# Seven products for the spatial gate's values, and convolution taps begun behind the first two tiles

## The reference, cut to what matters

```python
proj = rms_norm(h, g_mix_pre) @ w_in          # 1024 x 8192
z_sgu, z_conv, z_pool, z_gate = split(proj)   # 2048, 2048, 1024, 3072 columns

def spatial_gating(z, w_s, b_s, g_v, b_v):    # z = gelu(z_sgu)
    u, v = split(z, 2)
    v = layer_norm(v, g_v, b_v)               # v: 256 x 1024, the "values"
    return u * (w_s applied over tokens in blocks of 128 to v, plus b_s)

def conformer_conv(z, w_dw, b_dw, g_ln, b_ln):
    a, gate = split(z, 2)
    h = a * sigmoid(gate)
    h = depthwise causal convolution of h over tokens, 31 taps, + b_dw
    return silu(layer_norm(h, g_ln, b_ln))

def multiscale_pool(z, w_pool, s_pool):       # window means of 2, 4, 8, 16 tokens minus z,
    ...                                       # then four 256 x 256 products
merged = gate0 * (spatial @ w_sgu_out) + gate1 * (conv @ w_conv_out) + gate2 * (pool @ w_pool_out)
```

## Time and profile before

| | |
|---|---|
| median of 3 runs | 2272.47 us |
| profiled execution | 2274.29 us, span 2272.6 us |
| PE busy | 2067.7 us (91%) |
| DVE busy | 1442.3 us (63%) |
| POOL busy | 723.7 us (32%) |
| ACT busy | 699.2 us (31%) |

### The profile page before, as it was taken

The page is one execution under the profiler, slowest core; times in us unless marked ns, Lnnn a source line. Parts: engine busy times, 40 slices in busy tenths (PEclk is TensorE's granted clock), DMA queues, the critical chain, the costliest instruction groups (busy, mean ns, idle before and its releaser), DMA issues.

```text
span 2272.6 us, 21412 instructions
## 1 busy us (share of the span) xinstructions
PE 2067.7 (91%) x6060; PEld 1085.4 (48%) x6060; DVE 1442.3 (63%) x3261; ACT 699.2 (31%) x1517; POOL 723.7 (32%) x627
## 2 busy tenths in 40 slices
PE   9999999999999999999887878799899988887876
PEld 8864445455867555444332222276554444222222
DVE  3989777665551356667666666522766666666664
ACT  1013102111201214444434334423334344433442
POOL 1252420000000024544444445300254456444442
PEclk9999999999999999999999999999999999999999
DMA  6445444444545359999999999963699999999997
GB/s 230 148 150 186 160 162 148 167 167 169 185 166 211 132 226 374 421 422 421 422 422 421 422 422 422 416 243 139 265 421 421 421 422 421 421 422 422 422 421 323
DMA packets 98443, 703.07 MB, mean 309 GB/s; under 512 B 11136, under 2 KB 11648, under 8 KB 13248
## 3 DMA queue, kind: packets, MB, share of 16 engines
q0 software_dynamic: 73856, 537.17, 57.0%
q1 hardware_dynamic: 20016, 141.04, 17.3%
q10 hardware_dynamic: 4496, 23.92, 2.7%
HBM read 700.51 MB, written 1.05 MB: 309 GB/s over the span
## 4 chain that ended last, share of the span: by engine, by line
PE 44%; DMA 30%; ACT 5%; issue 4%; DVE 2%; POOL 1%; POOLq 0%; DVEq 0%; ACTq 0%; SPq 0%
DMA arena<-uv,expert_index 30%; PE aux L1008 13%; PE acc L573 9%; PE acc L538 7%; PE aux L538 5%; PE aux L857 3%; PE acc L1025 2%; PE acc L927 2%; ACT arena L1538 1%; ACT arena L1541 1%; ACT L1538 1%; POOL arena L1279 1%; ACT L1530 1%; DVE arena L2267 1%; PE acc L904 1%
## 5 line engine op out<-in xcount | busy, mean ns | idle before, releaser
L1008 PE MATMUL aux<-arena 128*128 128x512 f32 x2048 | 1002.7, 618 | 183.7 <-ACT arena L1541 180.3
L1279 POOL DMA_INDIRECT arena<-uv,expert_index x512 | 610.3, 1192 | 970.5 <-PE aux L1008 567.9
L2267 DVE SCALAR_TENSOR_TENSOR arena<-arena 128x1024 f32<-128x1024 f32 x512 | 632.4, 1235 | 412.9 <-DMA arena<-uv,expert_index 412.7
L1008 PEld LDWEIGHTS aux<-arena 128*128 128x128 f32 x2048 | 366.9, 192 | 721.1 <-ACT arena L1541 432.5
L1538 ACT ACTIVATE arena<-ident,dots 128x128 f32<-128x128 f32 x512 | 205.3, 401 | 701.9 <-DVE arena L2267 699.7
L573 PE MATMUL acc<-x,w_ring 128*128 128x256 f32 x1264 | 277.3, 382 | 2.5 <-DVE x L1709 2.3
L573 PEld LDWEIGHTS acc<-x,w_ring 128*128 128x128 f32 x1264 | 242.1, 192 | 36.7 <-DVE x L1709 2.5
L1541 ACT ACTIVATE arena<-arena,gate 128x128 f32<-128x128 f32 x512 | 205.5, 401 | 17.0
L1751 DVE TENSOR_TENSOR first_query_weights<-w_ring 128x1024 f32<-128x1024 f32 (+1 forms) x71 | 85.8, 1208 | 101.0 <-PE aux L538 90.3
L538 PE MATMUL acc<-first_query_weights,arena 128*128 128x512 f32 (+1 forms) x284 | 141.6, 581 | 0.1
L1793 DVE SCALAR_TENSOR_TENSOR arena<-arena,channel_vectors (+1 forms) x240 | 108.6, 531 | 0.2
(11 more groups left out here) (322 smaller groups left out, 1892.7 us busy)
## 6 DMA issues: line engine op xcount, KB each, us to landing
w_ring<-stream SPq DMA_DIRECT2D x133, 1024.0 KB, 4.8
arena<-uv,expert_index POOLq DMA_INDIRECT x512, 14.8
arena<-first_heads ACTq DMA_DIRECT2D x6, 1024.0 KB, 10.0
first_query_weights<-first_heads ACTq DMA_DIRECT2D x4, 1024.0 KB, 9.9
row_vectors<-rows ACTq DMA_DIRECT2D x3, 1024.0 KB, 13.0
scratch<-keys ACTq DMA_DIRECT2D x2, 1024.0 KB, 5.5
arena<-ret_out_held ACTq DMA_DIRECT2D x2, 1024.0 KB, 14.8
x<-first_heads ACTq DMA_DIRECT2D x2, 1024.0 KB, 4.8
```

What stands on the lines that cost most here:

```text
L1008: last = nc.tensor.matmul(AUX[2 * tt + c][:, :], DG[:, slot, :], G[:, row(layer, slot), D + c * 512:D + (c + 1) * 512], start=False, stop= ...
L1279: pool.indirect_dma_start(G[:, row(layer, s % RING), :], None, uv, bass.IndirectOffsetOnAxis(ap=EIDX[:, par, s:s + 1], axis=0),).then_inc( ...
L2267: v.scalar_tensor_tensor(G[:, row(layer, slot), 0:D], G[:, row(layer, slot), 0:D], 1.0, HTM[:, tt, :], ALU.mult, ALU.mult, accum_out=HD[:, ...
```

## The change

* `v` becomes the first seven-unit, number 0 (`SPATIAL_V`); all others move up by one (`GATE = 1`, `BRANCH = 4`). Its weight tiles are laid out for it.
* PE: `token_major(X1, KT, 2)` is replaced by four `seven_step`s, the first with order 5, 4, 3, 1, 6, 2, 7, waiting for the u banks to be stored; then it waits for `first_copied` and the unit's third `banks_read` ahead of the pool branch's products.
* ACT: four evacuations with Gelu from PSUM become `copy_first` and four Gelus in place in VT, as the additions come.
* DVE: the loop is written out, and its order changes: banks 0, 1; taps 0; banks 2, 3; taps 2 with banks 4, 5 ahead of its tap 16; banks 6, 7; taps 4; taps 6 with the values' combines 0, 1, 2 ahead of taps 4, 12 and 28; fold; combine 3 of the values; combine 0 of the first gate unit; `add_products` of the values; combines 1 to 3 of the first gate unit.
* POOL: two waits are renumbered to the same points of the work.

```diff
-SEVEN_UNITS = [(first_block("gates") + STEPS * u, STEPS, 512) for u in range(6)]
-BRANCH = 3
+SEVEN_UNITS = [(first_block("v"), STEPS, 512)]
+SPATIAL_V, GATE = 0, 1
+SEVEN_UNITS += [(first_block("gates") + STEPS * u, STEPS, 512) for u in range(6)]
+BRANCH = GATE + 3
...
-            token_major(X1, KT, 2)
+            u_uses = ring.n
+
+            def u_stored(bank):
+                ring.wait_stored(u_uses - BANKS + (bank - u_uses) % BANKS)
...
+            for j in range(STEPS):
+                seven_step(SPATIAL_V, j, X1, SPLIT_X, sums_from(0), None, None if j else u_stored)
             pe.wait_ge(pooled_ready, 1)
+            pe.wait_ge(first_copied, SPATIAL_V + 1)
+            pe.wait_ge(banks_read, 7 * SPATIAL_V + 3)
...
-            for c in range(2):
-                for tt in range(TT):
-                    evacuate_tm(ACT.Gelu_apprx_tanh, VT[:, tt, c * 512:(c + 1) * 512])
+            copy_first(SPATIAL_V)
+            for tt, c, read in PARTS:
+                act.wait_ge(banks_read, 7 * SPATIAL_V + read)
+                x = VT[:, tt, c * 512:(c + 1) * 512]
+                nc.scalar.activation(x, x, ACT.Gelu_apprx_tanh).then_inc(values_active, 1)
...
+            def glu(k, count):
+
+                for s in range(k, k + count):
+                    ring.wait_full()
+                    dve.wait_ge(gate_half, s + 1)
+                    ring.release(v.tensor_tensor(PADH[:, s, PAD:PAD + S], ring.bank()[:, 0:S], SG[:, s % BANKS, :], ALU.mult))
+                for u in range(ring.n - count, ring.n):
+                    ring.wait_stored(u)
+
             dve.wait_ge(pads_ready, 1)
-            with repeat(dve, 2, (ring, BANKS), (chain, 2 * CONV)) as i:
-                for s in range(BANKS):
-                    ring.wait_full()
-                    dve.wait_ge(gate_half, s + 1 + i * BANKS)
-                    ins = v.tensor_tensor(PADH[:, s + i * BANKS, PAD:PAD + S], ring.bank()[:, 0:S], SG[:, s, :], ALU.mult)
-                    ring.release(ins)
-                for u in range(ring.n - BANKS, ring.n):
-                    ring.wait_stored(u)
-                taps(i * 2)
+            glu(0, 2)
+            taps(0)
+            glu(2, 2)
+            taps(2, {16: lambda: glu(4, 2)})
+            glu(6, 2)
             taps(4)
 
-            taps(6, {8: 0, 16: 1, 24: 2})
-            combine(0, 3)
+            taps(6, {4: lambda: combine(SPATIAL_V, 0), 12: lambda: combine(SPATIAL_V, 1), 28: lambda: combine(SPATIAL_V, 2)})
+            fold(CV)
+            combine(SPATIAL_V, 3)
+            combine(GATE, 0)
+            add_products(SPATIAL_V, *(VT[:, tt, c * 512:(c + 1) * 512] for c in range(2) for tt in range(TT)))
+            for j in range(1, STEPS):
+                combine(GATE, j)
...
-    t += _tiles(w_in, _tm(list(seq(8, 16)), 8))
+    t += _tiles(w_in, _sevens(8, seq(8, 12), seq(12, 16)))
```

More of the change, by code:

```diff
@@ L350, in seven_results @@
         def seven_results(unit):
-            at = 25 if unit < FFN_IN else 55
+            at = 87 if unit == SPATIAL_V else 25 if unit < FFN_IN else 55
             return [AR[:, (at + 2 * j) * S:(at + 2 * j) * S + SEVEN_UNITS[unit][2]] for j in range(4)]
@@ L393, in build @@
         split_pool, gated = sem("split_pool"), sem("gated")
+        values_active = sem("values_active")
         mix_read, part_merged, merged_dve = sem("mix_read"), sem("part_merged"), sem("merged_dve")
@@ L671, in _, with sums_from @@
             pairs(X1, KT, 8)
-            token_major(X1, KT, 2)
+            u_uses = ring.n
+            def u_stored(bank):
+                ring.wait_stored(u_uses - BANKS + (bank - u_uses) % BANKS)
+            def sums_from(base):
+                return lambda j: pe.wait_ge(split_pool, base + j + 1)
+            for j in range(STEPS):
+                seven_step(SPATIAL_V, j, X1, SPLIT_X, sums_from(0), None, None if j else u_stored)
             pe.wait_ge(pooled_ready, 1)
+            pe.wait_ge(first_copied, SPATIAL_V + 1)
+            pe.wait_ge(banks_read, 7 * SPATIAL_V + 3)
             for g in range(4):
@@ L679, in pool_stored @@
                 ring.wait_stored(mixed_uses - BANKS + (bank - mixed_uses) % BANKS)
-            def sums_from(base):
-                return lambda j: pe.wait_ge(split_pool, base + j + 1)
             for u in range(3):
                 for j in range(STEPS):
-                    seven_step(u, j, X1, SPLIT_X, sums_from(0) if u == 0 else None, None,
-                               pool_stored if u == 0 and j == 0 else None)
+                    seven_step(GATE + u, j, X1, SPLIT_X, None, None, pool_stored if u == 0 and j == 0 else None)
                 if u == 1:
@@ L1214, in _ @@
                     pool.sem_inc(pooled_ready, 1)
-            for u in range(20, 24):
+            for u in range(16, 20):
                 pool.wait_ge(acc_free[u % BANKS], u // BANKS + 1)
-            pool.wait_ge(steps_done, STEPS)
+            pool.wait_ge(steps_done, SEVEN_STEP0[GATE + 1])
             for j in range(STEPS):
@@ L1349, in _, with copy_first @@
                 evacuate(ACT.Gelu_apprx_tanh, U[:, 2 * s:2 * s + 2, :])
-            for c in range(2):
-                for tt in range(TT):
-                    evacuate_tm(ACT.Gelu_apprx_tanh, VT[:, tt, c * 512:(c + 1) * 512])
+            def copy_first(unit):
+                u1 = seven_results(unit)[0]
+                act.wait_ge(product_ended, 5 * unit + 1)
+                nc.scalar.activation(u1, SEVEN[1][:, 0:SEVEN_UNITS[unit][2]], ACT.Copy).then_inc(first_copied, 1)
+            copy_first(SPATIAL_V)
[3 more added lines that the diff above has]
+                nc.scalar.activation(x, x, ACT.Gelu_apprx_tanh).then_inc(values_active, 1)
             for s in range(4):
@@ L1359, in _ @@
                                                   scale=col("s_pool", 2 * s + 1)))
[L1361 to L1365, removed]
             def gates(u):
-                copy_first(u)
+                copy_first(GATE + u)
                 for tt, c, read in PARTS:
-                    act.wait_ge(banks_read, 7 * u + read)
+                    act.wait_ge(banks_read, 7 * (GATE + u) + read)
                     x = GATES[u][:, 2 * tt + c, :]
@@ L1783, in taps @@
                         chain.wait_back(0)
-                        combine(0, between[k])
+                        between[k]()
                     for c in range(2):
@@ L1822, in add_gates @@
             def add_gates(u):
-                add_products(u, *(GATES[u][:, 2 * tt + c, :] for c in range(2) for tt in range(TT)))
+                add_products(GATE + u, *(GATES[u][:, 2 * tt + c, :] for c in range(2) for tt in range(TT)))
             def add_branch(u):
                 add_products(BRANCH + u, *(BRANCHES[u][:, 2 * tt + c, :] for c in range(2) for tt in range(TT)))
-            fold(CV)
-            ring.n += 8
+            ring.n += 8 + 4
             dve.wait_ge(rows_loaded, 16)
[L1831 to L1834, removed]
+            combine(GATE + 1, 0)
             add_gates(0)
-            combine(1, 1)
+            combine(GATE + 1, 1)
             centre(CV)
-            combine(1, 2)
+            combine(GATE + 1, 2)
             n["squares"] += 6
@@ L1841, in _ @@
             fold(SC)
-            combine(1, 3)
+            combine(GATE + 1, 3)
+            dve.wait_ge(values_active, 4)
             norm_values(0)
-            combine(2, 0)
+            combine(GATE + 2, 0)
             add_gates(1)
-            combine(2, 1)
-            combine(2, 2)
+            combine(GATE + 2, 1)
+            combine(GATE + 2, 2)
             layer_scale(CV, EPS)
-            combine(2, 3)
+            combine(GATE + 2, 3)
             combine(BRANCH, 0)
```

## The result

The kernel after takes 2285.63 us (median of 5 runs, 2283.37 to 2288.41), the kernel before 2271.99 us in the same series: ratio 1.0057, 95% interval 1.0046 to 1.0067, which is 12.9 us slower (10.5 to 15.2). The forecast was 2286.6 us. The profiled execution took 2284.61 us, span 2282.9.

What follows compares the result with a forecast made beforehand. PE, busy 91% of the span, bounds the kernel; 3.4 us saved, 17.1 lost waiting for DVE's combines and 0.4 to the clock make +14.1 on 2272.47, so 2286.6 us; range 2279 to 2291.

Steps and rivals of the forecast that it cites:

- PE saves 3.43 us if it never waits: In v's products on PE: 28 products instead of 32 take 24.04 us for 27.47, 3.43 saved without waits.
- DVE is the bound from 31 us on: DVE's convolution and combines: no idle time from 31.85 to 163 us, last tap group beginning at 109.4.
- Taps beside pooling cost 1.316: DVE's last tap group beside POOL's pooling: 1.316 us per slowed tap against 0.397 alone, 0.92 extra.
- POOL goes through: Pooling beside DVE's taps: POOL's instructions keep their 1.26 us whether DVE runs or not, and DVE pays.
- Combine beside pooling 5.5: The values' combine 0 on DVE during pooling: 5.5 us for 2.60 alone, from up to 3 x 0.95 more.
- Combine 1, 2, 3 end at 140.6, 155.9, 163.2: The values' later combines on DVE end at these us, against 134.1, 146.6 and 161.9 wanted by PE.
- Waits of 6.5, 9.3, 1.3: PE waits for the values' combines 1, 2 and 3 by these us, 17.1 lost in all.
- the clock's 0.4: PE's lowered clock behind its stalls in v adds 0.4 us to v's end, bounds 0 and 2.3.
- +14.1 at the pool branch: V's end and the pool branch's start on PE: 168.8 us against 154.68, 14.1 us later.
- Nothing behind V absorbs or adds: Everything after v's products moves along with the shift: change 0 us, bounds -1 to +1.
- POOL's first pooling row ends at the end of the third group: POOL's first pooling instruction lasts until DVE's third tap group ends, about 110 us, then turns begin.
- The main rival: DVE's last tap group: turns with pooling cost no extra, one PE stall of 0.6 us, 2269.7 us; chance 0.07.

Runs made afterwards that it cites:

- experiment 4: Kernel after with DVE's combines moved ahead of most taps of the last tap group, same work otherwise; 2268.66 us, ratio to before 0.9982.
- experiment 6: Kernel before with the convolution loop written out and begun behind two banks, v still by eight products; 2271.90 us, ratio 0.9996.
- experiment 3: Kernel after with the old convolution loop back on DVE, so seven products without the early taps; 2300.75 us, ratio 1.0130.
- experiment 1: Kernel after with GpSimd's 18 pooling instructions left out and the pooled tile zeroed at the start; 2268.74 us, ratio to before 0.9981.
- experiment 5: Kernel after with one DVE wait for its last tap put ahead of tap 24 of the third tap group; 2286.93 us, ratio 1.0061.
- 8: Kernel after with idle 128x128 products filling PE's two long waits, 18 in step 1 and 36 in step 2; 2283.85 us, ratio 1.0045.
- experiment 2: Kernel before with GpSimd's 18 pooling instructions left out and the pooled tile zeroed at the start; 2272.29 us, ratio 1.0003.

## Why the prediction was right

The mechanism and its place were as forecast: DVE, slowed by the pooling, has the combines ready too late, and PE waits. The sum met the measurement within 1 us (2286.6 for 2285.63). That it came so close is in part luck: two terms were off in opposite directions, and the split of the loss over the steps was wrong. By its steps:

* *PE saves 3.43 us if it never waits*: shown by experiment 4: 3.4 in the time, 3.2 at the branch, behind a wait of 0.23.
* *DVE is the bound from 31 us on*: idle column empty. Each step between a bank's product and the next tap was sized 0.54, from the looped code's row; written out, it takes 31.50 - 31.38 = 0.12 (0.12 in experiment 6 too, while experiment 3 with the loop has 0.54). With three more such places, which take 0.84 to 0.87 us with their two products for the 1.3 that I took, the last group begins at 107.77, not 109.4. This is the term that was mis-sized most.
* *Taps beside pooling cost 1.316*: 8.10 / 6 = 1.35 from 110.10 to 118.20. *POOL goes through*: nearly; in the turns its rows of 128x512 last 1.32 to 1.35 and beside a combine 1.60, for 1.26 alone. *Combine beside pooling 5.5*: 123.28 - 118.20 = 5.08; the 0.95 taken from the merging's row was a little high.
* *Combine 1, 2, 3 end at 140.6, 155.9, 163.2*: 138.9, 154.3, 161.7. All about 1.6 early, the offset of the last group.
* *Waits of 6.5, 9.3, 1.3*: 5.16, 6.48 and none. Here the working was loose: it listed waits as if PE ran at full pace between them and added the clock's 0.4 at the end. In truth the low clock behind the first wait (2.89) eats into the second, 6.48 + 2.89 = 9.37, and that behind the second (2.04) replaces the third: step 3's second product starts at 162.4, 0.7 beyond combine 3 at 161.7 (the forecast said 0.5 and took 0.4). The total was nearly the same, as DVE set it.
* *+14.1 at the pool branch*: +12.9. The 1.2 between them are combine 3, 1.5 early, less the 0.3 that the clock cost more. The third addition ended 1.3 ahead of the need (0.9 forecast). `pooled_ready` came at 132.4, earlier than the 135 to 160 forecast, and nothing hung on it. *Nothing behind V absorbs or adds*: +12.5 at the first gather.
* *POOL's first pooling row ends at the end of the third group*: it ends 0.95 us behind the group's last tap (108.68 and 107.73), as before (123.51 and 122.56).

The main rival, that the turns would not cost as before, came nearly true where the pooling was left out (2269.7 forecast for it, 2268.74 in experiment 1). That DVE would wait for POOL's whole instruction did not show: 1.35 per tap, where the rule of the Trainium skill (SBUF — State Buffer, "SBUF: two separate sides") makes 1.67, an estimate from the tap's 0.397 and POOL's 1.27. What did show are turns, one DVE instruction for one of POOL's; but as the two together last longer than 1.35, they overlap in part, and the runs do not show a wholly exclusive lock.

## What to carry to other kernels

Before work of a full engine is traded for work of another, add up what the other must deliver by which time, at the price that it pays beside its present neighbours: 18 GpSimd instructions that nobody waited for cost 16 to 17 us, once DVE had no slack under them, and nothing while it had. What counts is the order: the same instructions with the combines ahead of the taps turned +12.9 into -3.4 us. And halves of a change can be worth nothing or be harmful alone (0, +28.7 us) and still both be needed.

## What the runs showed of the hardware that was not expected

* A run of taps without a break holds POOL's instruction off for as long as it lasts, 22.95 us, 8.36 in the kernel after; a single wait of DVE for its own last instruction ends that (2.81 in experiment 5). From then on they alternate one by one, although nothing else is changed in the taps. Why the one state doesn't pass into the other was not tried.
* Waits of 5.2 and 6.5 us on PE lowered the granted clock to its 1.2 GHz level for part of the stretches behind them and made six products of 128x512 2.89 and 2.04 us longer.
* In the profiled executions of experiments 1, 6 and 8 the conv products began at 16.8 for 14.7 us. The row that grew is the sum of squares ahead of them; here it is in experiment 6 (16 rows took 3.72 us in the kernels before and after):

```profile
6.43 5.79 PE L643 MATMUL aux<-scratch,ones 128*128 128x256 f32 x16 [0.72 <-ACT scratch L1336]
```

Experiments 6 and 8 change nothing there, and experiment 2, with the same zeroed tile as experiment 1, has 3.72; so two profiles are best compared from an event at the front, not from the start of the span.
